# Odd stage of a two-layer trunk: gate products spread through the next projection, as three passes over high and low halves

## The chip, the cores and the metric

The kernel runs on 1 core of one Trainium2 chip. The metric is the device time of one execution in microseconds (us). An engine here is TensorE (PE in the rows, with its weight loads as PEld), VectorE (DVE), ScalarE (ACT), GpSimd (POOL) or SyncE (SP, which issues DMAs). Every engine runs its own instructions in order, and a wait holds back all that stands behind it on that engine.

## What is computed

Two layers follow each other; the change is in the mixer of the second (odd) one, a gated linear recurrence over 1,040 positions and 1,280 channels. `h` is the output of the layer before. Around it stand the even mixer (convolution and sparse attention) and, after each mixer, a routed expert layer and a layer norm; the change leaves them alone.

```python
def rg_lru(xr, w_a, b_a, w_x, b_x, lam):
    xb = xr.reshape(bsz, length, RNN_BLOCKS, RNN_BLOCK_W)          # 10 blocks of 128 channels
    r = sigmoid(einsum('blnc,ncd->blnd', xb, w_a) + b_a)
    i = sigmoid(einsum('blnc,ncd->blnd', xb, w_x) + b_x)
    log_a = -RG_C * r * softplus(-lam)
    a = exp(log_a)
    u = sqrt(-expm1(2.0 * log_a)) * (i * xr)
    ...                                                            # h[n] = a[n] * h[n-1] + u[n]

def rglru_mixer(h, w_in, conv_w, conv_b, w_a, b_a, w_x, b_x, lam, w_out):
    gate, xr = jnp.split(h @ w_in, 2, axis=-1)
    xr = causal_depthwise_conv(xr, conv_w, conv_b)                 # width 4
    y = rg_lru(xr, w_a, b_a, w_x, b_x, lam)
    return (jax.nn.gelu(gate) * y) @ w_out
```

## The kernel before

The stage is `gated_recurrence`. Channels lie on the 128 partitions and positions in the free dimension. The input projection is cut into 20 tiles of 128 output channels (`ODD_TILES`): for each of the 10 channel blocks t one tile of `xr` (s = 1) and one of `gate` (s = 0). Tile 0 is `xr` of block 0, tile 2t+1 is `xr` of block t+1, tile 2t+2 is `gate` of block t. A tile is 72 matmuls of 348 columns: three thirds of the positions, eight pieces of the contraction, and three passes each (`mm3`: high weights by high rows, high by low, low by high), since weights and rows are held as two fp32r halves, high and low.

What each engine does for block t, in the order of its own instructions:

- SP loads the weights of a tile into `raw`, two tiles ahead (line 2323).
- ACT writes the high half of a tile's weights (`split_hi`, line 2364), copies a projected `xr` tile out of PSUM (`take`, line 2373) or runs GeLU on a `gate` tile (line 2375), runs the six sigmoids of the gates (line 2384), then tanh and two exponentials (`decays`, lines 2392 to 2395), and, once DVE has made its input, the square root (`root`, line 2399). It loads an activation table before the first sigmoid, the first exponential, the square root and the GeLU.
- DVE writes the low half of the weights (`split_lo`, line 2432), makes the width-4 convolution of the next block (`conv(t + 1)`, lines 2445 and 2447), then the factor under the root (line 2475, the words below call it e), the product with the gated input (line 2456) and the scan (line 2457).
- POOL multiplies the input gate by the convolved rows (`gated`, line 2485) and the scanned rows by the GeLU output (`out`, line 2490).
- PE projects the tiles in order. After tile 2t+1 stand the gate products of block t (`gates`, line 2345): six matmuls in plain fp32, three thirds of the positions by two gates, from the convolved rows `rg_xc` and the weights `rg_w`. Each waits for the sigmoid two before it, since the PSUM tile `rg_ps` has two buffers. In the trace each of these six stands as two matmul records. Then tile 2t+2 follows.

The order is written out by hand on each engine; nothing reorders it. Semaphores link the engines: `tile_mm` (a tile is projected), `taken` (a tile was copied out), `hi_done` and `lo_done` (weight halves), `conv_d` (convolution done), `gate_mm` and `sig_d` (gate product and sigmoid done), `ix_d`, `h_d`, `y_d`.

Of the kernel before, what the change touches and what calls it, by code (L numbers as in the profile page):

```python
# [14 lines left out]
ALU = mybir.AluOpType  # L15
ACT = mybir.ActivationFunctionType
# [2280 lines left out]
GATE_UNITS = [(j, a0, min(TC, T - a0)) for j in range(2) for a0 in range(0, T, TC)]  # L2297


def gated_recurrence(nc, hT_hi, hT_lo, w_pairs_d, raw, w_loaded, wab, wab_loaded, rp, gate):  # L2300
# [4 lines left out]
    with Ctx(nc) as c:  # L2305
# [3 lines left out]
        sp_, sp8 = c.sb("rg_sp", [P, 3 * RT]), c.sb("rg_sp8", [P, 3 * RT])  # L2309
# [5 lines left out]
            c.sem("rg_" + n) for n in ("cd", "mm", "sg", "ad", "ed", "sq", "ix", "h", "y"))  # L2315
        block = c.block()
# [9 lines left out]
        def _(pe):  # L2326
            def project(n):
                b = n % 2
                pe.wait_ge(lo_done, n + 1)
                if n >= 2:  # L2330
                    pe.wait_ge(taken, n - 1)
                for j in range(3):
                    for k in range(KC):
                        w, m = slice(k * P, (k + 1) * P), slice(j * TC, (j + 1) * TC)
                        last = mm3(pe, ps[b][:, j, 0:TC], (w_hi[:, b, w], w_lo[:, b, w]),
                                   (hT_hi[:, k, m], hT_lo[:, k, m]), k == 0, k == KC - 1)
                last.then_inc(tile_mm, 1)

            def gates(t):
                pe.wait_ge(conv_d, t + 1)  # L2340
                for i, (j, a0, n) in enumerate(GATE_UNITS):
                    u = t * NU + i
                    if u >= 2:
                        pe.wait_ge(sig_d, u - 1)
                    pe.matmul(g_ps[u % 2][:, 0:n], wab[:, j * RT + t, :], xc[:, t % 2, a0:a0 + n], start=True, stop=True
                              ).then_inc(gate_mm, 1)

            project(0)
            project(1)
            pe.wait_ge(wab_loaded, 16)  # L2350
            gates(0)
            for t in range(1, RT):
                project(2 * t)
                project(2 * t + 1) if t + 1 < RT else None
                gates(t)
            project(NT - 1)

        @block.scalar
        def _(act):
# [6 lines left out]
            def take(n):  # L2366
# [7 lines left out]
                else:  # L2374
                    act.activation(gate[:, t, :].rearrange("p (j n) -> p j n", j=3), src, ACT.Gelu_apprx_tanh).then_inc(taken, 1)

# [32 lines left out]
            act.activation(sp_[:, 0:RT], sp_[:, RT:2 * RT], ACT.Ln, bias=1.0).then_inc(lam_d, 1)  # L2409
            take(0)  # L2410
            split_hi(2)
            act.wait_ge(neg_d, 3)
            for t in range(RT):
# [5 lines left out]
                if t + 1 < RT:  # L2419
                    take(2 * t + 1)  # L2420
                    split_hi(2 * t + 3)
                decays(t)
                root(t)
            take(NT - 1)

        @block.vector
        def _(dve):
# [250 lines left out]
```

## Time and profile before

| | |
|---|---|
| median of 3 runs | 2745.87 us (2743.52 to 2746.61) |
| profiled execution, its own time | 2740.98 us |
| its span, first to last instruction | 2739.2 us |
| PE busy, PEld busy | 2470.9 us (90%), 2098.1 us (77%) |
| DVE, ACT, POOL busy | 2015.1 (74%), 1699.7 (62%), 653.5 us (24%) |
| odd stage, in the span | 1575.4 to 1872.2 us |
| mean granted clock of TensorE | 0.943 |

A page of the profile gives, per engine, the share of the span in which it was busy. The span is a chain of stages with different limits, so the averages say little of the odd stage. It is read from windows of its own, from the instructions in order of time, and from the list of who waited for whom. Times in the rows are us from the start of the span; durations of a single matmul overlap those of the next, so the distance between two starts is what a matmul costs in a stream. The other stages take the rest of the span and hold no line that the change touches, but for two small constants whose place in memory moves.

### The profile page before, as it was taken

The page shows a single profiled execution, that of the slowest core. Times are in us where ns is not written, and L with a number is a line of the kernel's source. Part 1 is how long each engine was busy: PE and PEld are TensorE (multiplying, and loading weights), DVE is VectorE, ACT ScalarE, POOL GpSimd, SP SyncE. Part 2 cuts the span into 40 slices and gives each one's busy share as a digit, 9 for nine tenths or more (in the row PEclk, how much of TensorE's full clock was granted, in tenths as well). Part 3 has the DMA queues.
Part 4 walks back from the last instruction along what each step waited for, and adds up shares of the span by engine and source line. Part 5 has one row for each costly group of instructions (what it writes and reads, how often), then busy time and mean ns, then how long its engine had stood idle before and what let it go on. Part 6 is the DMA issues. An engine that isn't in the chain of part 4 may idle for free. (4 is left out here: it accounts for less than half of the span.)

```text
span 2739.2 us, 37516 instructions
## 1 busy us (share of the span) xinstructions
PE 2470.9 (90%) x12571; PEld 2098.1 (77%) x12571; DVE 2015.1 (74%) x2325; ACT 1699.7 (62%) x1800; POOL 653.5 (24%) x484
## 2 busy tenths in 40 slices
PE   8889987998895999999999499997959999999993
PEld 8779966886684888888888388886848888888882
DVE  4677775668658898888988535455469888988895
ACT  2367845666314777777777355554137787787773
POOL 0105716653001212122121311121011222122223
PEclk9899998998996999999999699999969999999996
DMA  5502233322437879998798410103247789999994
GB/s 171 125 1 93 78 96 92 85 57 56 143 116 281 311 262 365 362 382 287 284 368 308 179 47 31 39 24 125 93 171 295 286 294 371 368 365 366 376 355 146
DMA packets 115273, 565.16 MB, mean 206 GB/s; under 512 B 23520, under 2 KB 27872, under 8 KB 65904
## 3 DMA queue, kind: packets, MB, share of 16 engines
q1 hardware_dynamic: 89776, 512.15, 51.2%
q0 software_dynamic: 25408, 51.84, 7.0%
q8 instruction: 53, 0.87, 0.1%
q14 instruction: 36, 0.29, 0.0%
HBM read 574.22 MB, written 74.34 MB: 237 GB/s over the span
## 5 line engine op out<-in xcount | busy, mean ns | idle before, releaser
L1967 DVE TENSOR_TENSOR e0wlo<-e0raw,e0whi 128x2048 fp32r<-128x2048 f32 x214 | 486.7, 2289 | 68.9 <-ACT e0whi L1815 68.8
L1967 DVE TENSOR_TENSOR e1wlo<-e1raw,e1whi 128x2048 fp32r<-128x2048 f32 x208 | 472.8, 2288 | 66.0 <-ACT e1whi L1815 65.8
L1815 ACT ACTIVATE e0whi<-e0raw 128x2048 fp32r<-128x2048 f32 x214 | 409.9, 1916 | 103.8 <-PE e0u L90 42.1
L1815 ACT ACTIVATE e1whi<-e1raw 128x2048 fp32r<-128x2048 f32 x208 | 398.3, 1915 | 101.0 <-PE e1u L90 40.0
L88 PE MATMUL odd_ps<-h2T_hi,odd_w_hi 128*128 128x348 f32 x480 | 158.3, 330 | 6.2 <-DVE odd_w_lo L2432 6.2
L89 PE MATMUL odd_ps<-h2T_lo,odd_w_hi 128*128 128x348 f32 x480 | 155.6, 324 | 0.0
L90 PE MATMUL odd_ps<-h2T_hi,odd_w_lo 128*128 128x348 f32 x480 | 155.3, 324 | 0.0
L88 PE MATMUL m_y<-m_whi,m_xhi 128*128 128x512 f32 (+1 forms) x304 | 121.6, 400 | 21.7 <-DVE m_wlo L1547 21.0
L89 PE MATMUL m_y<-m_wlo,m_xhi 128*128 128x512 f32 (+1 forms) x304 | 119.8, 394 | 0.0
L90 PE MATMUL m_y<-m_whi,m_xlo 128*128 128x512 f32 (+1 forms) x304 | 119.7, 394 | 0.0
L88 PE MATMUL e0g<-e0whi,e0xh 128*128 128x512 f32 x284 | 115.6, 407 | 0.7 <-DVE e0xl L1972 0.7
L88 PE MATMUL e0u<-e0whi,e0xh 128*128 128x512 f32 x292 | 115.6, 396 | 0.0
L89 PE MATMUL e0u<-e0wlo,e0xh 128*128 128x512 f32 x292 | 115.5, 395 | 0.0
L90 PE MATMUL e0u<-e0whi,e0xl 128*128 128x512 f32 x292 | 115.5, 395 | 0.0
L723 ACT ACTIVATE act_junk<-score,cand 128x656 bf16<-128x656 f32 (+2 forms) x96 | 96.8, 1010 | 28.9 <-DVE cand L710 22.5
L2432 DVE TENSOR_TENSOR odd_w_lo<-odd_w_raw,odd_w_hi 128x1024 fp32r<-128x1024 f32 x20 | 28.4, 1423 | 116.6 <-ACT odd_w_hi L2364 116.6
L88 PE MATMUL e0yp<-e0whi,e0hh 128*128 128x512 f32 x280 | 113.8, 407 | 0.0
L88 PE MATMUL e1u<-e1whi,e1xh 128*128 128x512 f32 x284 | 112.4, 396 | 0.0
L90 PE MATMUL e0g<-e0whi,e0xl 128*128 128x512 f32 x284 | 112.3, 396 | 0.0
L89 PE MATMUL e1u<-e1wlo,e1xh 128*128 128x512 f32 x284 | 112.3, 395 | 0.0
L90 PE MATMUL e1u<-e1whi,e1xl 128*128 128x512 f32 x284 | 112.3, 395 | 0.0
L89 PE MATMUL e0g<-e0wlo,e0xh 128*128 128x512 f32 x284 | 112.2, 395 | 0.0
(456 smaller groups left out, 7089.8 us busy)
## 6 DMA issues: line engine op xcount, KB each, us to landing
e0raw<-in_moe_w_gate SPq DMA_DIRECT2D x72, 1024.0 KB
e0raw<-in_moe_w_up SPq DMA_DIRECT2D x72, 1024.0 KB
e0raw<-in_moe_w_down SPq DMA_DIRECT2D x72, 1024.0 KB
e1raw<-in_moe_w_gate SPq DMA_DIRECT2D x70, 1024.0 KB
e1raw<-in_moe_w_up SPq DMA_DIRECT2D x70, 1024.0 KB
e1raw<-in_moe_w_down SPq DMA_DIRECT2D x70, 1024.0 KB
qki_w_raw<-in_w_even SPq DMA_DIRECT2D x22, 512.0 KB, 5.2
odd_w_raw<-in_w_odd SPq DMA_DIRECT2D x20, 512.0 KB, 3.7
```

What stands on the lines that cost most here:

```text
L88: pe.matmul(out, stat[0], mov[0], start=start, stop=False)
L89: pe.matmul(out, stat[0], mov[1], start=False, stop=False)
L90: return pe.matmul(out, stat[1], mov[0], start=False, stop=stop)
L723: act.activation(junk[:, at:at + WIDTH[b]], score[:, AT[b]:AT[b] + WIDTH[b]], ACT.Sign, scale=-1.0, bias=self.cand[:, n:n + 1].bitcast(F32 ...
L1815: act.activation(w_hi[:, i, :], raw[:, i, :], ACT.Copy).then_inc(hi_done[i], 1)
L1967: dve.tensor_tensor(w_lo[:, i, :], raw[:, i, :], w_hi[:, i, :].bitcast(F32), ALU.subtract).then_inc(lo_done[i], 1)
L2432: dve.tensor_tensor(w_lo[:, n % 2, :], raw[:, n % 2, :], w_hi[:, n % 2, :].bitcast(F32), ALU.subtract).then_inc(lo_done, 1)
```

## The change

Two things are done to the gate products of block t, and two tiles are split for it.

- The six products are no longer plain fp32 in a row of their own. Each is now an `mm3` of three fp32r passes, and they stand inside the projection of tile 2t+1: one after every second group of three matmuls, so after groups 2, 4, ... 12 of its 24. For block 0 they stand in tile 1 after groups 14 to 24, for block 9 in tile 19 (the last) after groups 1 to 6. Where block t's products stood behind tile 2t+1 before, they now stand inside it.
- ACT gets `xc_high(t)`: the high half of the block's gate weights (128x256) and of its convolved rows (128x1040). For block t+1 it stands behind `root(t)`, ahead of the GeLU tile.
- DVE gets `xc_low(t)`: two subtractions of 128x128 and one of 128x1040, the low halves. For block t+1 it stands behind the scan of block t, ahead of the low half of the next weights.
- `conv` no longer waits for the gate products of the block two before it but for `xc_high` of it, since that is what reads `rg_xc` now.
- The small tiles `rg_sp` and `rg_sp8` move into unused columns of `const`, and `conv_b` and `lnp` live only in the first layer, which makes room for the four new tiles.

```diff
@@ -2295,9 +2295,10 @@
 
 ODD_TILES = [(0, 1)] + [tile for t in range(RT) for tile in ((t + 1, 1), (t, 0)) if tile[0] < RT]
 GATE_UNITS = [(j, a0, min(TC, T - a0)) for j in range(2) for a0 in range(0, T, TC)]
-
-
-def gated_recurrence(nc, hT_hi, hT_lo, w_pairs_d, raw, w_loaded, wab, wab_loaded, rp, gate):
+GATE_EVERY, FIRST_GATE = 2, 12
+
+
+def gated_recurrence(nc, hT_hi, hT_lo, w_pairs_d, raw, w_loaded, wab, wab_loaded, rp, gate, spare):
 
 
     B_A, B_X, LAM, CB, CW = 0, RT, 2 * RT, 3 * RT, 4 * RT
@@ -2306,13 +2307,16 @@
         w_hi, w_lo = c.sb("odd_w_hi", [P, 2, KC * P], F32R), c.sb("odd_w_lo", [P, 2, KC * P], F32R)
         xr = c.sb("xr", [P, 2, RCONV - 1 + TP])
         xc, a, tt, rr, ii = (c.sb("rg_" + n, [P, 2, T]) for n in ("xc", "a", "t", "r", "i"))
-        sp_, sp8 = c.sb("rg_sp", [P, 3 * RT]), c.sb("rg_sp8", [P, 3 * RT])
+        xc_hi, xc_lo = (c.sb("rg_xc_" + n, [P, T], F32R) for n in ("hi", "lo"))
+        wab_hi, wab_lo = (c.sb("rg_w_" + n, [P, 2, P], F32R) for n in ("hi", "lo"))
+        sp_, sp8 = (spare[:, a * RT:(a + 3) * RT] for a in (0, 3))
         ps = [c.ps(f"odd_ps{s}", [P, 3, 512]) for s in range(2)]
         g_ps = [c.ps(f"rg_ps{s}", [P, 512]) for s in range(2)]
         hi_done, lo_done, tile_mm, taken = (c.sem("odd_" + n) for n in ("hi", "lo", "mm", "taken"))
         lam_d, neg_d, zero_d, chain = (c.sem("rg_" + n) for n in ("lam", "neg", "z", "ch"))
         conv_d, gate_mm, sig_d, act_d, e_d, sq_d, ix_d, h_d, y_d = (
             c.sem("rg_" + n) for n in ("cd", "mm", "sg", "ad", "ed", "sq", "ix", "h", "y"))
+        xc_hi_done, xc_lo_done = (c.sem("rg_" + n) for n in ("xc_hi", "xc_lo"))
         block = c.block()
 
         @block.sync
@@ -2326,6 +2330,7 @@
         def _(pe):
             def project(n):
                 b = n % 2
+                t = 0 if n == 1 else n // 2 if n % 2 else None
                 pe.wait_ge(lo_done, n + 1)
                 if n >= 2:
                     pe.wait_ge(taken, n - 1)
@@ -2334,26 +2339,26 @@
                         w, m = slice(k * P, (k + 1) * P), slice(j * TC, (j + 1) * TC)
                         last = mm3(pe, ps[b][:, j, 0:TC], (w_hi[:, b, w], w_lo[:, b, w]),
                                    (hT_hi[:, k, m], hT_lo[:, k, m]), k == 0, k == KC - 1)
+                        i, between = divmod(j * KC + k + 1 - (FIRST_GATE if t == 0 else 0), 1 if n == NT - 1 else GATE_EVERY)
+                        if t is not None and between == 0 and 1 <= i <= NU:
+                            gate_unit(t, i - 1)
                 last.then_inc(tile_mm, 1)
 
-            def gates(t):
-                pe.wait_ge(conv_d, t + 1)
-                for i, (j, a0, n) in enumerate(GATE_UNITS):
-                    u = t * NU + i
-                    if u >= 2:
-                        pe.wait_ge(sig_d, u - 1)
-                    pe.matmul(g_ps[u % 2][:, 0:n], wab[:, j * RT + t, :], xc[:, t % 2, a0:a0 + n], start=True, stop=True
-                              ).then_inc(gate_mm, 1)
-
-            project(0)
-            project(1)
-            pe.wait_ge(wab_loaded, 16)
-            gates(0)
-            for t in range(1, RT):
-                project(2 * t)
-                project(2 * t + 1) if t + 1 < RT else None
-                gates(t)
-            project(NT - 1)
+            def gate_unit(t, i):
+                j, a0, n = GATE_UNITS[i]
+                if t == 0 and i == 0:
+                    pe.wait_ge(wab_loaded, 16)
+                if i == 0:
+                    pe.wait_ge(xc_hi_done, 2 * t + 2)
+                    pe.wait_ge(xc_lo_done, 3 * t + 3)
+                u, w = t * NU + i, j * RT + t
+                if u >= 2:
+                    pe.wait_ge(sig_d, u - 1)
+                mm3(pe, g_ps[u % 2][:, 0:n], (wab_hi[:, j, :], wab_lo[:, j, :]),
+                    (xc_hi[:, a0:a0 + n], xc_lo[:, a0:a0 + n]), True, True).then_inc(gate_mm, 1)
+
+            for n in range(NT):
+                project(n)
 
         @block.scalar
         def _(act):
@@ -2374,6 +2379,13 @@
                 else:
                     act.activation(gate[:, t, :].rearrange("p (j n) -> p j n", j=3), src, ACT.Gelu_apprx_tanh).then_inc(taken, 1)
 
+            def xc_high(t):
+                act.wait_ge(conv_d, t + 1)
+                if t:
+                    act.wait_ge(gate_mm, NU * t)
+                act.activation(wab_hi[:], wab[:, t:RT + t + 1:RT, :], ACT.Copy).then_inc(xc_hi_done, 1)
+                act.activation(xc_hi[:], xc[:, t % 2, :], ACT.Copy).then_inc(xc_hi_done, 1)
+
             def sigmoids(t):
                 if t >= 2:
                     act.wait_ge(h_d, t - 1)
@@ -2407,8 +2419,10 @@
             act.activation(sp_[:, RT:2 * RT], sp_[:, 0:RT], ACT.Exp, scale=-1.0).then_inc(lam_d, 1)
             act.wait_ge(lam_d, 3)
             act.activation(sp_[:, 0:RT], sp_[:, RT:2 * RT], ACT.Ln, bias=1.0).then_inc(lam_d, 1)
+            act.wait_ge(wab_loaded, 16)
             take(0)
             split_hi(2)
+            xc_high(0)
             act.wait_ge(neg_d, 3)
             for t in range(RT):
                 if t:
@@ -2421,6 +2435,8 @@
                     split_hi(2 * t + 3)
                 decays(t)
                 root(t)
+                if t + 1 < RT:
+                    xc_high(t + 1)
             take(NT - 1)
 
         @block.vector
@@ -2438,7 +2454,7 @@
                 dve.wait_ge(taken, tile + 1)
                 if t >= 2:
                     dve.wait_ge(ix_d, t - 1)
-                    dve.wait_ge(gate_mm, NU * (t - 1))
+                    dve.wait_ge(xc_hi_done, 2 * (t - 1))
                 for j in range(RCONV):
                     src, wj = xr[:, s, j:j + T], rp[:, CW + RT * j + t:CW + RT * j + t + 1]
                     if j == 0:
@@ -2448,6 +2464,13 @@
                     if j < RCONV - 1:
                         ch.link(ins)
                 ins.then_inc(conv_d, 1)
+
+            def xc_low(t):
+                dve.wait_ge(xc_hi_done, 2 * t + 2)
+                for j in range(2):
+                    dve.tensor_tensor(wab_lo[:, j, :], wab[:, j * RT + t, :], wab_hi[:, j, :].bitcast(F32), ALU.subtract
+                                      ).then_inc(xc_lo_done, 1)
+                dve.tensor_tensor(xc_lo[:], xc[:, t % 2, :], xc_hi[:].bitcast(F32), ALU.subtract).then_inc(xc_lo_done, 1)
 
             def scan(t):
                 s = t % 2
@@ -2466,6 +2489,7 @@
             dve.wait_ge(zero_d, 1)
             conv(0)
             split_lo(2)
+            xc_low(0)
             for t in range(RT):
                 if t + 1 < RT:
                     split_lo(2 * t + 3)
@@ -2474,6 +2498,8 @@
                 dve.wait_ge(act_d, 3 * t + 3)
                 dve.scalar_tensor_tensor(tt[:, t % 2, :], rr[:, t % 2, :], 1.0, tt[:, t % 2, :], ALU.add, ALU.mult).then_inc(e_d, 1)
                 scan(t)
+                if t + 1 < RT:
+                    xc_low(t + 1)
                 if t + 2 < RT:
                     split_lo(2 * t + 4)
 
@@ -2506,12 +2532,13 @@
-        cb, lnp, rp = g.sb("conv_b", [P, CG]), g.sb("lnp", [P, 2 * CG]), g.sb("rp", [P, 8 * RT])
+        rp = g.sb("rp", [P, 8 * RT])
+            cb, lnp = c.sb("conv_b", [P, CG]), c.sb("lnp", [P, 2 * CG])
@@ -2580,7 +2607,7 @@
-                gated_recurrence(nc, hT_hi, hT_lo, A["w_odd"], odd_raw, odd_loaded, wab, wab_loaded, rp, gate)
+                gated_recurrence(nc, hT_hi, hT_lo, A["w_odd"], odd_raw, odd_loaded, wab, wab_loaded, rp, gate, const[:, C_PHASE:C_ALL])
```

On PE, before: the end of tile 3 (`xr` of block 2), the gate products of block 1, the start of tile 4.

```order
L90 MATMUL odd_ps1<-h2T_hi,odd_w_lo 128x348
L2345 MATMUL rg_ps0<-rg_xc,rg_w 128x348
L2345 MATMUL rg_ps1<-rg_xc,rg_w 128x348
L2345 MATMUL rg_ps0<-rg_xc,rg_w 128x344
L2345 MATMUL rg_ps1<-rg_xc,rg_w 128x348
L2345 MATMUL rg_ps0<-rg_xc,rg_w 128x348
L2345 MATMUL rg_ps1<-rg_xc,rg_w 128x344
L88 MATMUL odd_ps0<-h2T_hi,odd_w_hi 128x348
```

On PE, now: the start of tile 3, with the gate products of block 1 in it.

```order
L90 MATMUL odd_ps0<-h2T_hi,odd_w_lo 128x348
L88 MATMUL odd_ps1<-h2T_hi,odd_w_hi 128x348
L89 MATMUL odd_ps1<-h2T_lo,odd_w_hi 128x348
L90 MATMUL odd_ps1<-h2T_hi,odd_w_lo 128x348
L88 MATMUL odd_ps1<-h2T_hi,odd_w_hi 128x348
L89 MATMUL odd_ps1<-h2T_lo,odd_w_hi 128x348
L90 MATMUL odd_ps1<-h2T_hi,odd_w_lo 128x348
L88 MATMUL rg_ps0<-rg_xc_hi,rg_w_hi 128x348
L89 MATMUL rg_ps0<-rg_xc_lo,rg_w_hi 128x348
L90 MATMUL rg_ps0<-rg_xc_hi,rg_w_lo 128x348
L88 MATMUL odd_ps1<-h2T_hi,odd_w_hi 128x348
```

The first gate product of block 1 stood behind all 72 matmuls of tile 3 and now stands behind six of them; the other 66 are queued behind its wait.

On DVE, before, one block from the low halves of the weights (`odd_w_lo`) through the convolution (`rg_xc`), e (`rg_t` from `rg_r`), the product (`rg_i`) and the scan (`rg_t` from `rg_a`):

```order
L2432 TENSOR_TENSOR odd_w_lo<-odd_w_raw,odd_w_hi 128x1024 x2
L2445 TENSOR_SCALAR rg_xc<-xr,rp 128x1040
L2447 SCALAR_TENSOR_TENSOR rg_xc<-xr,rp,rg_xc 128x1040 x3
L2475 SCALAR_TENSOR_TENSOR rg_t<-rg_r,rg_t 128x1040
L2456 TENSOR_TENSOR rg_i<-rg_i,rg_t 128x1040
L2457 SCALAR_TENSOR_TENSOR rg_t<-rg_a,rg_i 128x1040
```

On DVE, now:

```order
L2448 TENSOR_TENSOR odd_w_lo<-odd_w_raw,odd_w_hi 128x1024 x2
L2461 TENSOR_SCALAR rg_xc<-xr,rp 128x1040
L2463 SCALAR_TENSOR_TENSOR rg_xc<-xr,rp,rg_xc 128x1040 x3
L2499 SCALAR_TENSOR_TENSOR rg_t<-rg_r,rg_t 128x1040
L2479 TENSOR_TENSOR rg_i<-rg_i,rg_t 128x1040
L2480 SCALAR_TENSOR_TENSOR rg_t<-rg_a,rg_i 128x1040
L2471 TENSOR_TENSOR rg_w_lo<-rg_w,rg_w_hi 128x128 x2
L2473 TENSOR_TENSOR rg_xc_lo<-rg_xc,rg_xc_hi 128x1040
```

The three subtractions for the gate products (`rg_w_lo`, `rg_xc_lo`) stand behind e, the product and the scan, though their input is the convolution ahead of these.

On ACT, now, from the input's copy of a tile (`xr`) to the GeLU:

```order
L2378 ACTIVATE xr<-odd_ps 128x1044
L2369 ACTIVATE odd_w_hi<-odd_w_raw 128x1024
L2404 ACTIVATE rg_t<-rg_r,const 128x1040
L2405 ACT_TABLE_LOAD
L2405 ACTIVATE rg_a<-rg_r,const 128x1040
L2407 ACTIVATE rg_r<-rg_r,const 128x1040
L2411 ACT_TABLE_LOAD
L2411 ACTIVATE rg_t<-rg_t 128x1040
L2386 ACTIVATE rg_w_hi<-rg_w 128x256
L2387 ACTIVATE rg_xc_hi<-rg_xc 128x1040
L2380 ACT_TABLE_LOAD
L2380 ACTIVATE gate<-odd_ps 128x1044
```

(Line numbers of these rows are those of the changed kernel.) Before, the rows of lines 2386 and 2387 were not there, and GeLU's followed the square root. The high halves stand behind the root, which waits for DVE's e.

## Rows read from the trace of the kernel before

**Rows 1.** The page: engine, busy us (share of the span) xinstructions.
```profile
PE 2470.9 (90%) x12571; PEld 2098.1 (77%) x12571; DVE 2015.1 (74%) x2325; ACT 1699.7 (62%) x1800; POOL 653.5 (24%) x484
```

**Rows 2.** Windows: length, busy us (xinstructions) by engine, clock granted, DMA share, GB/s.
```profile
1608.50:1835.10 226.60, 216.37 (x1251) 200.10 (x1250) 112.20 (x72) 133.66 (x145) 43.21 (x15) 1.00 0.11 36
...
1715.60:1744.05 28.45, 27.00 (x158) 24.99 (x157) 14.28 (x9) 16.67 (x18) 5.81 (x2) 1.00 0.11 37
```

**Rows 3.** PE in order of time: start, us, instruction, xcount, [idle before <-releaser].
```profile
1583.16 0.33 PE L88 MATMUL odd_ps<-h2T_hi,odd_w_hi 128*128 128x348 f32 x1
...
1588.42 0.33 PE L88 MATMUL odd_ps<-h2T_hi,odd_w_hi 128*128 128x348 f32 x1
...
1591.78 0.32 PE L88 MATMUL odd_ps<-h2T_hi,odd_w_hi 128*128 128x348 f32 x1
```

**Rows 4.** PE in order of time around gates(3), after gates(0); last weight loads of gates(3), gates(8).
```profile
1687.30 1.33 PE L2345 MATMUL rg_ps<-rg_xc,rg_w 128*128 128x348 f32 x4
1690.03 2.92 PE L2345 MATMUL rg_ps<-rg_xc,rg_w 128*128 128x344 f32 x8 [1.39 <-ACT rg_r L2384]
1692.52 0.58 PE L88 MATMUL odd_ps<-h2T_hi,odd_w_hi 128*128 128x348 f32 x1
1692.94 0.32 PE L89 MATMUL odd_ps<-h2T_lo,odd_w_hi 128*128 128x348 f32 x1
...
1608.48 0.58 PE L88 MATMUL odd_ps<-h2T_hi,odd_w_hi 128*128 128x348 f32 x1
...
1692.10 0.30 PEld L2345 LDWEIGHTS rg_ps<-rg_xc,rg_w 128*128 128x128 f32 x2 [0.29 <-ACT rg_i L2384]
...
1834.37 0.30 PEld L2345 LDWEIGHTS rg_ps<-rg_xc,rg_w 128*128 128x128 f32 x2 [0.29 <-ACT rg_i L2384]
```

**Rows 5.** DVE in order of time, block 0's convolution, then one later block.
```profile
1593.13 0.82 DVE L2445 TENSOR_SCALAR rg_xc<-xr,rp 128x1040 f32<-128x1040 f32 x1 [11.86 <-ACT xr L2373]
1593.98 3.98 DVE L2447 SCALAR_TENSOR_TENSOR rg_xc<-xr,rp,rg_xc 128x1040 f32<-128x1040 f32 x3
1597.88 1.22 DVE L2432 TENSOR_TENSOR odd_w_lo<-odd_w_raw,odd_w_hi 128x1024 fp32r<-128x1024 f32 x1
...
1695.44 1.69 DVE L2432 TENSOR_TENSOR odd_w_lo<-odd_w_raw,odd_w_hi 128x1024 fp32r<-128x1024 f32 x1 [12.81 <-ACT odd_w_hi L2364]
1697.06 2.96 DVE L2445 TENSOR_SCALAR rg_xc<-xr,rp 128x1040 f32<-128x1040 f32 x1
1703.95 1.23 DVE L2475 SCALAR_TENSOR_TENSOR rg_t<-rg_r,rg_t 128x1040 f32<-128x1040 f32 x1
1706.39 1.24 DVE L2456 TENSOR_TENSOR rg_i<-rg_i,rg_t 128x1040 f32<-128x1040 f32 x1 [1.21 <-ACT rg_t L2399]
1707.67 2.32 DVE L2457 TENSOR_TENSOR_SCAN rg_t<-rg_a,rg_i 128x1040 f32<-128x1040 f32 x1
```

**Rows 6.** ACT in order of time: block 0's copy out, then the same later block.
```profile
1591.97 1.04 ACT L2373 ACTIVATE xr<-odd_ps 128x1044 f32<-128x1044 f32 x1 [11.26 <-PE odd_ps L90]
...
1693.43 1.04 ACT L2373 ACTIVATE xr<-odd_ps 128x1044 f32<-128x1044 f32 x1
1694.35 1.06 ACT L2364 ACTIVATE odd_w_hi<-odd_w_raw 128x1024 fp32r<-128x1024 f32 x1
...
1705.22 1.07 ACT L2399 ACTIVATE rg_t<-rg_t 128x1040 f32<-128x1040 f32 x1 [3.77 <-DVE rg_t L2475]
```

**Rows 7.** POOL in order of time, the same later block.
```profile
1693.61 2.44 POOL L2485 TENSOR_TENSOR rg_i<-rg_i,rg_xc 128x1040 f32<-128x1040 f32 x1 [22.64 <-ACT rg_i L2384]
1696.01 3.45 POOL L2490 TENSOR_TENSOR gate<-rg_t,gate 128x1040 f32<-128x1040 f32 x1
...
1869.74 2.38 POOL L2490 TENSOR_TENSOR gate<-rg_t,gate 128x1040 f32<-128x1040 f32 x1 [7.20 <-ACT gate L2375]
```

**Rows 8.** Small operations on DVE and ACT, in order of time.
```profile
1580.75 0.17 DVE L2463 TENSOR_TENSOR rg_sp<-rg_sp 128x10 f32<-128x10 f32 x1 [1.83 <-ACT rg_sp L2409]
...
1578.98 0.21 ACT L2407 ACTIVATE rg_sp<-rg_sp 128x10 f32<-128x10 f32 x1
```

**Rows 9.** SP's queue: the load of the gates' weights.
```profile
1538.06 0.44 SPq L2579 DMA_DIRECT2D rg_w<-in_w_rg  x1
```

**Rows 10.** PE's idle times, and windows of the clock behind the second.
```profile
307.73 0.43 PE L88 MATMUL qkg_ps<-hT_hi,qki_w_hi 128*128 128x348 f32 x1 [3.03 <-POOL qki_w_lo L219]
...
1852.81 4.22 PE L2345 MATMUL rg_ps<-rg_xc,rg_w 128*128 128x344 f32 x8 [4.92 <-ACT rg_r L2384]
...
307.70:312.00 4.30, 4.27 (x27) 4.28 (x28) 3.57 (x13) 4.30 (x7) 1.37 (x1) 1.00 0.97 229
...
1852.80:1856.20 3.40, 3.39 (x6) 1.88 (x7) 0.00 (x0) 1.50 (x3) 0.00 (x0) 0.51 0.00 0
```

## The prediction

> **What bounds the kernel now.** The page of the profile comes first: PE is busy 90% of the span and its weight loads 77% [rows 1], so what lengthens or shortens PE's stream moves the end one for one, unless a wait takes its place. The change lies in the odd stage alone, so windows come next: from block 1's first tile to the end of block 8's gate products the stage takes 226.6 us at a granted clock of 1.00, and one block after another takes 28.45 us, with DVE busy 14.3 and ACT 16.7 of that [rows 2]. Nothing but PE is near its limit over a block. What matters is then the order within a block, so I read the engines in order of time.
>
> PE: eleven groups of three matmuls lie between the two starts at 1583.16 and 1588.42, so one matmul of a stream costs 5.26 / 33 = 0.159 us [rows 3]. A block has 144 of them, 23.0 us. The rest of the 28.45 is the gate products: their first start is 1687.30 and the next tile starts at 1692.52, 5.22 us, and that tile's first matmul takes 0.42 instead of 0.16 to hand over (1692.52 to 1692.94), which makes 5.5 [rows 4]. In them lies one idle time of 1.39 us, behind the first sigmoid.
>
> **The change, part by part.** I call B the start of the matmul behind the last one of tile 2t+1.
>
> *Gate products on PE.* Removed: 5.5 us a block. Added: 6 products of 3 passes, 18 x 0.159 = 2.9 us, taking fp32r passes of 348 columns at the price of the tile's own. If nothing waits, a block is 162 x 0.159 = 25.8 us, 2.6 less than 28.45.
>
> *The wait that goes with it.* The products of block t+1 now stand behind only 72 + 6 matmuls after B, so PE asks for them at B + 78 x 0.159 = B + 12.4. What they need is the last low half of `xc_low(t + 1)`. Its chain, each step from a row:
> - ACT copies the tile out from B + 0.2 (1591.97 against the next tile's start at 1591.78) [rows 3, 6]. The six sigmoids end ahead of B now, so nothing is ahead of it.
> - From the start of the copy to that of DVE's low half of the weights: 1693.43 to 1695.44, 2.0 us, ACT's two operations [rows 5, 6]. B + 2.2.
> - Low half and convolution: in a late block 1695.44 to 1703.95, 8.5 us, e following [rows 5]. Two of these are long because POOL is at work: the low half takes 1.69 against 1.22, the first step of the convolution 2.96 against 0.82, and POOL's product ends at 1696.05 and its next operation at 1699.46 [rows 5, 7]. In the change the sigmoids end some 5 us ahead of B, and POOL's two operations, 2.4 each without a neighbour [rows 7], are over by then. So 8.5 - 0.5 - 2.1 = 5.9. If that cover is gone, the 2.6 come back.
> - e 1.23, root 1.07, product 1.24, scan 2.32: from 1703.95 to the end of the scan at 1709.99, 6.0 us [rows 5, 6]. B + 14.1.
> - `xc_low`: two subtractions of 128x128, between 0.17 (128x10) and 1.22 (128x1024); I take 0.28, on the line between them, as 128 columns are nearer to 10. One of 128x1040 at 1.24, as the product [rows 5, 8]. 1.8 in all, B + 15.9. Bounds: 1.6 to 3.6.
> - The high halves on ACT, a copy of 256 columns between 0.21 and 1.06 (0.45 taken) and one of 1040 at 1.06 [rows 6, 8], end at B + 12: the root ends at B + 10.4, 3.7 before the scan does. They are hidden, until they took over 3.7 us; GeLU and the next weights behind them wait for nothing urgent, as tile 2t+3 ends over 13 us later.
>
> So `xc_low` stands behind the root and the scan of the block before, which it doesn't need, and PE waits from B + 12.4 to B + 16.0, 3.5 us, with 66 matmuls of the tile and 18 passes queued behind that wait. These take 84 x 0.159 = 13.4 and the start after the idle time 0.1: the block is 29.45 us, 1.0 more than before. The 3.5 idle eat the 2.6 won. Within the tile the products then come every 9 matmuls, 1.43 us; the first sigmoid and its table load take some 1.8, against 2.9 until the third product, so no second wait.
>
> *Ends of the stage.* Block 0: the convolution ends at 1597.9 [rows 5], ACT's halves at 1599.5, `xc_low` at 1601.3. PE asks after 42 matmuls of tile 1, 1591.78 + 6.7 = 1598.5: 2.8 idle, then 48 matmuls; tile 2 starts at 1609.1 against 1608.48 [rows 3, 4]: +0.6. The block after it: the last products of block 0 stand at the very end of tile 1, so its last sigmoid, POOL's product and the copy come 1 us late, 30.45. Eight blocks after: 30.45 + 7 x 29.45 = 236.6. Before, tile 18 starts 0.42 after the last weight load of its gate products, as tile 14 does, at 1834.8: 226.3 from 1608.48 [rows 4]. +10.3. Block 9: the products follow after every group, the wait is 4.0 and a second one behind the table load 0.6; its sigmoids, exponentials, root, scan and POOL's last product end 35.8 after B, and before it was 1872.1 - 1834.8 = 37.3 [rows 7]: -1.5. At no cost: the new room in memory; ACT's new wait for the gates' weights, issued 54 us before it needs them [rows 9]; and SP's loads, which wait for DVE's low half of tile 2t+2. That stands behind `xc_low` now and ends at B + 17.1, and the tile it loads for is split over 20 us later.
>
> The sum is +0.6 + 10.3 - 1.5 = +9.4 us.
>
> **The clock.** PE will have ten new idle times: 2.8, 4.5 (block 1, with its late copy), eight of 3.5 to 4.0. The rows have two of that size: after 3.03 idle the granted clock stayed 1.00, after 4.92 it was 0.51 over the next 3.4 us, level 1.2 GHz [rows 10]. Such a fall costs half of 3.4, 1.7 us, and all of it on the path, since PE's tile sets the next block. Ours lie between the two rows. I take two falls, the longest waits, +3.4, and keep none and nine (+15.3) as bounds.
> The Trainium skill ("TensorE: Matmul & The Clock Gate", section "Why this matters for your kernels") warns of idle gaps between bursts of matmuls, since the engine goes back to its lower clock. By that rule every one of our waits but the shortest costs its 1.7 us and the time is that of rival 1; the 3.03 row does not show it and the 4.92 row does.
>
> Against the profiled execution: 2740.98 + 9.4 + 3.4 = 2753.8. It lies 4.9 under the median of the runs, so against the median: 2745.87 + 12.8 = **2758.7 us**, +0.5%.
>
> **Rivals.**
> 1. *The clock falls after nearly every wait.* For it: 3.5 to 4.5 is above 3.03. Against: it is 1.4 under 4.92. Nine falls: 2745.87 + 9.4 + 15.3 = 2770.6, or 2778 if a low stretch is longer than 3.4 us.
> 2. *The products are ready in time, and the change does what it says* (on the other side: faster). The gain is decided at one place, the first product's wait in tiles 3 to 17: the chain must be under 12.4 us instead of 15.9. Then each block is 25.8, 2.6 x 8 = 21 less, 2.4 less in tile 1 and about 5 at the end: 2745.87 - 28 = 2718. For it: only if e, root and scan didn't stand ahead of `xc_low`; they do, and their 6.0 us are measured [rows 5, 6].
> 3. *Wait and gain cancel.* If the chain were 0.9 us shorter, or three waits less exposed, a block stays 28.45 and the time moves within 0.2%: 2745.87 - 1 to + 5. For it: 6 or 7 steps of mine come from a block in which POOL and the sigmoids lay otherwise. Against: all the low ends together take 0.2 off the chain.
>
> **How the numbers follow.** Forecast (no fall to five falls, 2753 to 2765) 0.55; rival 1 (2765 to 2778) 0.20; rival 3 (2741 to 2751) 0.14; rival 2 (about 2718) 0.08; longer still, if the small subtractions go by their upper bound (+1.8 a block), 0.03. A range from 2748 to 2775 leaves out rival 2, about half of rival 3 and the top of rival 1, some 0.2. A measurement of this kernel tells 0.2% (5.5 us) from no change. Faster than that: rival 2 and a little of rival 3, 0.09. Within: 0.13. Slower: 0.78.
>
> **What the changed profile would show.** Right: PE idle 3 to 4 us ahead of the first product in tiles 3 to 17, put down to DVE's low half of the rows; a block of 29 to 30 us; POOL's two operations ahead of the copy; the convolution's first step at 0.8; some windows of clock 0.5 to 0.9 behind these waits, or none. Wrong: no wait at that product and a block near 26 (rival 2), a wait under 2.7 (rival 3), a low clock in each block (rival 1), a long first step of the convolution (POOL's cover gone), or passes in the tile that cost more than 0.159.

## The result and the profile after

| | before | after |
|---|---|---|
| median of 4 runs | 2744.69 us | 2761.28 us (2760.0 to 2764.31) |
| ratio, 95% interval | | 1.0074 (1.0061 to 1.0086) |
| span of the profiled execution | 2739.2 | 2760.0 |
| odd stage, first matmul to POOL's last product | 294.3 | 316.1 |
| one block in the middle of the stage | 28.45 | 30.77 |

The kernel became slower by 0.7%. In the profiled executions the odd stage is 21.8 us longer. The two executions differ elsewhere too: the stage before ends 0.6 us later and the stages behind take 1.7 us less. Over all the profiles below, the odd stage starts between 1574.5 and 1583.2 us though nothing ahead of it differs, so the whole time of a single execution is good to some microseconds. A stage measured within itself is good to about one: its first tile runs in part at a low clock in every profile, for 3.6 to 6.2 us, and that differs from profile to profile. Time and stage stand side by side for that reason.

The page has PE as busy as before [rows 1]; DVE and POOL are a little less busy, ACT 13 us more:

```profile
PE 2471.8 (90%) x12631; PEld 2116.2 (77%) x12631; DVE 2010.1 (73%) x2355; ACT 1713.0 (62%) x1820; POOL 639.9 (23%) x484
```

The windows, with columns as in [rows 2]: from the last product of block 0 to the end of block 8 (block 1's first tile starts 0.5 us into it, at 1609.78), one block, and the 3.4 us and 15.2 us from the start of that block's products.

```profile
1609.31:1857.76 248.45, 221.92 (x1302) 219.89 (x1301) 106.51 (x96) 145.50 (x161) 40.98 (x17) 0.94 0.10 32
1703.95:1734.72 30.77, 27.57 (x165) 27.32 (x164) 13.25 (x12) 18.14 (x20) 4.81 (x2) 0.94 0.10 35
1719.70:1723.10 3.40, 3.37 (x15) 3.40 (x16) 1.07 (x1) 2.23 (x3) 0.00 (x0) 0.66 0.35 105
1719.70:1734.90 15.20, 15.17 (x86) 15.20 (x87) 1.07 (x1) 4.58 (x7) 4.81 (x2) 0.89 0.11 36
```

Where [rows 2] had a granted clock of 1.00 over eight blocks, it is 0.94 now, and 0.66 right behind the wait. PE in order of time in that block:

```profile
1716.22 0.32 PE L90 MATMUL odd_ps<-h2T_hi,odd_w_lo 128*128 128x348 f32 x1
1719.73 0.40 PE L88 MATMUL rg_ps<-rg_xc_hi,rg_w_hi 128*128 128x348 f32 x1 [3.20 <-issue]
...
1721.59 0.49 PE L88 MATMUL rg_ps<-rg_xc_hi,rg_w_hi 128*128 128x348 f32 x1
1721.88 0.49 PE L89 MATMUL rg_ps<-rg_xc_lo,rg_w_hi 128*128 128x348 f32 x1
...
1724.20 0.34 PE L88 MATMUL rg_ps<-rg_xc_hi,rg_w_hi 128*128 128x344 f32 x1
```

The block's tile boundary B is 1703.95. PE runs to 1716.22 + 0.16, asks for the first product at B + 12.4, and gets it at 1719.73, B + 15.8. The list of waits calls the idle time "issue" and names no engine; in `e3_fill` below it puts the same wait down to DVE's low half of the rows, `rg_xc_lo`. At 1721.6 two matmuls are 0.29 us apart, which is the 1.2 GHz level (0.16 at 2.4). DVE and ACT in that block:

```profile
1706.16 1.23 DVE L2448 TENSOR_TENSOR odd_w_lo<-odd_w_raw,odd_w_hi 128x1024 fp32r<-128x1024 f32 x1 [16.16 <-ACT odd_w_hi L2369]
1707.31 0.82 DVE L2461 TENSOR_SCALAR rg_xc<-xr,rp 128x1040 f32<-128x1040 f32 x1
1712.05 1.23 DVE L2499 SCALAR_TENSOR_TENSOR rg_t<-rg_r,rg_t 128x1040 f32<-128x1040 f32 x1
1714.50 1.24 DVE L2479 TENSOR_TENSOR rg_i<-rg_i,rg_t 128x1040 f32<-128x1040 f32 x1 [1.21 <-ACT rg_t L2411]
1715.77 2.32 DVE L2480 TENSOR_TENSOR_SCAN rg_t<-rg_a,rg_i 128x1040 f32<-128x1040 f32 x1
1718.01 0.47 DVE L2471 TENSOR_TENSOR rg_w_lo<-rg_w,rg_w_hi 128x128 fp32r<-128x128 f32 x2
1718.40 1.23 DVE L2473 TENSOR_TENSOR rg_xc_lo<-rg_xc,rg_xc_hi 128x1040 fp32r<-128x1040 f32 x1
...
1714.30 0.40 ACT L2386 ACTIVATE rg_w_hi<-rg_w 128x256 fp32r<-128x256 f32 x1
1714.60 1.06 ACT L2387 ACTIVATE rg_xc_hi<-rg_xc 128x1040 fp32r<-128x1040 f32 x1
```

The last low half ends at 1719.63 and PE starts at 1719.73. Against [rows 5] the first step of the convolution takes 0.82 instead of 2.96: POOL is out of its way, with operations of 2.44 and 2.42 us from 1729.81 to 1734.6, just ahead of the next boundary at 1734.72.

### The profile page after: what moved, and what is told of

Same layout as the page of the kernel before. It is cut to its first block and busy times, and to the rows that moved or that the text cites. A ratio compares the mean times of both kernels' runs of the same rounds, so it can differ in the third digit from the quotient of the medians.

```text
span 2760.0 us, 37696 instructions
## 1 busy us (share of the span) xinstructions
PE 2471.8 (90%) x12631; PEld 2116.2 (77%) x12631; DVE 2010.1 (73%) x2355; ACT 1713.0 (62%) x1820; POOL 639.9 (23%) x484
```

## The experiments

Two theories stood at the start. **A**: PE waits for a chain on ACT and DVE that ends 15.8 us behind the boundary, and each such wait brings PE's clock down, which costs time on top of the wait. **B**: the passes inside a tile cost more than 0.159 us each, or something else slows the 84 matmuls behind the wait; the idle time is only beside it. Each kernel was timed in 3 rounds (the last in 5) against the kernel before on the same chip. "Stage" is again from the first matmul of the odd stage to POOL's last product in the profiled execution: 294.3 before, 316.1 with the change. Times of different rows were taken beside different runs of the kernel before (medians 2739.9 to 2744.7), so the ratio is what to compare.

| kernel | time, us | ratio to before (95%) | stage, us | a block, us |
|---|---|---|---|---|
| the change | 2761.28 | 1.0074 (1.0061 to 1.0086) | 316.1 | 30.75 |
| e1_late | 2725.56 | 0.9942 (0.9925 to 0.9959) | 283.3 | 26.5 |
| e2_halves_first | 2738.11 | 0.9993 (0.9983 to 1.0003) | 292.4 | 27.8, two of 29.3 |
| e3_fill | 2748.18 | 1.0027 (1.0018 to 1.0037) | 303.3 | 29.27 |
| e4_two_later | 2749.27 | 1.0039 (1.0024 to 1.0053) | 305.9 | 28.27 and 29.80 |
| e5_passes_alone | 2742.22 | 1.0002 (0.9989 to 1.0014) | 296.0 | 28.0, one of 29.6 |
| e6_spread_alone | 2721.58 | 0.9929 (0.9911 to 0.9946) | 276.4 | 26.72 |
| e7_first_and_later | 2721.29 | 0.9920 (0.9902 to 0.9938) | 272.8 | 25.77 |
| e8_sigmoids_first | 2728.97 | 0.9948 (0.9929 to 0.9966) | 284.5 | 27.0 |
| e9_all | 2724.86 | 0.9943 (0.9924 to 0.9961) | 278.4 | 27.0 |
| e10_best | 2714.21 | 0.9891 (0.9875 to 0.9908) | 269.0 | 25.77 |

### The clock: fill the wait, or shorten it

`e3_fill` keeps the wait and gives PE something to do in it, FILL = 14 matmuls (code cut):

```diff
+                if i == 0:
+                    if t:
+                        for _ in range(FILL):
+                            pe.matmul(g_ps[u % 2][:, 0:TC], w_hi[:, 1, 0:P], hT_hi[:, 0, 0:TC], start=True, stop=True)
+                    pe.wait_ge(xc_hi_done, 2 * t + 2)
+                    pe.wait_ge(xc_lo_done, 3 * t + 3)
```

> The changed kernel with 14 more matmuls of 348 columns ahead of the wait of each block but the first, into the PSUM tile that the product then overwrites: 2.2 us of work in the idle 3.2 us, used by nobody. Theory (idle time brings the clock down, 1.3 us each in nine blocks): the idle time is 1.0, the clock stays at 1.00, a block of 29.4 us instead of 30.75, time about 2750. Rival (the slow 84 matmuls behind the wait have another cause): the same 30.75 and 2761. If filling delays the product: over 2761.

`e4_two_later` asks for the products two groups, 0.95 us, later:

```diff
-                        i, between = divmod(j * KC + k + 1 - (FIRST_GATE if t == 0 else 0), ...
+                        i, between = divmod(j * KC + k + 1 - (FIRST_GATE if t == 0 else 2), ...
```

> The products of blocks 1 to 9 stand two groups later (4 to 14, and 3 to 8 in the last tile), so PE asks 0.95 us later for the same chain. Theory: idle 2.25 us, the clock stays, a block of 28.45 us, time about 2742. Rival 1 (the clock falls after these waits too): a block of 29.8, about 2753. Rival 2 (the clock plays no part, only the place does): 0.95 a block, about 2753 with a clock of 1.00.

One block of `e3_fill` as a window and the list's line for its ten waits (us in total, times, longest), then two neighbouring blocks of `e4_two_later`:

```profile
1695.22:1724.50 29.28, 28.26 (x179) 28.00 (x178) 13.25 (x12) 18.02 (x20) 4.81 (x2) 1.00 0.12 37
...
PE rg_ps L88 <- DVE rg_xc_lo L2476: 13.2, 10, 2.6
```

```profile
1670.90:1699.16 28.26, 26.01 (x165) 25.75 (x164) 13.26 (x12) 18.03 (x20) 4.83 (x3) 1.00 0.12 38
1699.16:1728.95 29.79, 27.55 (x164) 27.29 (x163) 13.25 (x12) 18.14 (x20) 4.87 (x3) 0.94 0.11 36
```

More work for nothing made the kernel faster by 13 us: with 1.0 us idle instead of 3.2 the clock stays at 1.00 in blocks 2 to 9 and a block takes 29.27 instead of 30.75. So a fall costs 1.5 us, and theory B has no place left: the same passes behind the same chain run at full speed. The 1.5 comes out of the matmuls too: a low stretch of 3.4 us holds about 12 of them at 0.29 us, and 12 x (0.29 - 0.159) = 1.6. `e4_two_later` was expected to have no falls at an idle time of 2.25; it has them in about every second block, and the pair above shows the same 1.5 (29.79 against 28.26). So the time came out between the 2742 of the theory and the 2753 of rival 1, and what failed is the idea that 2.25 us are short enough.

Over the odd stages of all twelve profiles, PE's idle times by size and how many of them had a fall of the clock in or within 2 us behind them: 0.9 to 1.0 us, none of 24; 1.4 to 1.5, 2 of 17; 1.8 to 1.9, 3 of 8; 2.2 to 2.4, 5 of 9; 2.6 to 2.8, 6 of 10; 3.2, 8 of 8; over 3.6, 4 of 4. In these runs the share with a fall grows with the idle time. The Trainium skill ("TensorE: Matmul & The Clock Gate", section "Why this matters for your kernels") has it as a rule to keep such gaps short; the trace of the change agrees, with all nine waits of 3.2 us and more, and the shorter waits of `e4_two_later` show that it can strike earlier. The wait of 3.03 us in another stage, which had none [rows 10], stands in all twelve profiles at 2.9 to 3.0 us, in code that is the same in all of them but for places in memory. Eight of the twelve have a fall at it, and the kernel before is one of the four that have none. In `e1_late`, PE's row and the clock behind it:

```profile
303.94 0.43 PE L88 MATMUL qkg_ps<-hT_hi,qki_w_hi 128*128 128x348 f32 x1 [3.01 <-POOL qki_w_lo L219]
...
305.40:308.90 3.50, 3.50 (x14) 3.50 (x13) 2.97 (x9) 3.50 (x7) 2.03 (x1) 0.51 0.83 236
```

The clock falls at the same wait in one execution and not in another, so a single row without a fall could not tell that a wait of that size is safe.

### The place: ask later

`e1_late` has the products of every block at groups 14 to 24 (block 9: 10 to 15).

```diff
-                        i, between = divmod(j * KC + k + 1 - (FIRST_GATE if t == 0 else 0), ...
+                        i, between = divmod(j * KC + k + 1 - (FIRST_GATE if n < NT - 1 else 9), ...
```

> Only the place of the gate products changes: behind groups 14 to 24 of a tile for every block (as for block 0), behind groups 10 to 15 in the last tile. Theory (PE waits for a chain that ends 15.8 us behind the tile boundary, and a wait over 3 us brings the clock down): the products now come 18 us behind the boundary, so no wait and no low clock in blocks 1 to 8, a block of 25.8 us, time about 2724. Rival (the passes inside a tile cost more than 0.159 us, which would explain the 15.0 us behind the wait as well): no wait, but a block of 27.3, about 2736. If the late sigmoids push the next chain back by more than 2 us: a wait again, about 2745.

The direction and most of the size came: 14.4 us faster than before, and by the ratios 36 us under the change. But a block takes 26.5 and 0.5 us of wait are left, not 25.8 and none. DVE and POOL in one block (B = 1685.11) show why:

```profile
1688.24 1.69 DVE L2448 TENSOR_TENSOR odd_w_lo<-odd_w_raw,odd_w_hi 128x1024 fp32r<-128x1024 f32 x1 [9.29 <-ACT odd_w_hi L2369]
1689.86 2.96 DVE L2461 TENSOR_SCALAR rg_xc<-xr,rp 128x1040 f32<-128x1040 f32 x1
...
1686.41 2.44 POOL L2511 TENSOR_TENSOR rg_i<-rg_i,rg_xc 128x1040 f32<-128x1040 f32 x1 [20.67 <-ACT rg_i L2396]
1688.80 3.45 POOL L2516 TENSOR_TENSOR gate<-rg_t,gate 128x1040 f32<-128x1040 f32 x1
```

The products at the tile's end push the sigmoids over the boundary. POOL then runs beside the next convolution, the long 1.69 and 2.96 of [rows 5] are back, the price that the prediction had named for the lost cover, and the chain ends 19.2 us behind B instead of 15.8.

### The queues: take the halves ahead

`e2_halves_first` leaves the products where the change has them and moves the halves ahead of the root and of the scan.

```diff
                 decays(t)
-                root(t)
                 if t + 1 < RT:
                     xc_high(t + 1)
+                root(t)
...
-                scan(t)
                 if t + 1 < RT:
                     xc_low(t + 1)
+                scan(t)
```

> The products stay where the change put them; ACT's high halves move ahead of the root and DVE's low halves ahead of the product and the scan. Theory: the chain ends 11.2 us behind the boundary instead of 15.8, PE asks at 12.4, no wait in blocks 1 to 8 and hardly one in block 9, a block of 25.8 us, the 2.6 us wait of block 0 stays, time about 2720. Rival (the order on DVE does not matter, another wait is behind PE's): still 3 us idle and about 2761.

The wait for the rows' low half is gone in blocks 1 to 9, as the theory had it (the low half ends at B + 11.3), but the time is that of before (the interval of the ratio, 0.9983 to 1.0003, includes 1). The list of PE's waits in the odd stage names another engine (us in total, times, longest):

```profile
PE rg_ps L88 <- ACT rg_r L2396: 17.2, 9, 2.7
```

PE's row and ACT's queue ahead of it, in one block (B = 1696.93):

```profile
1714.14 0.42 PE L88 MATMUL rg_ps<-rg_xc_hi,rg_w_hi 128*128 128x344 f32 x1 [1.76 <-ACT rg_r L2396]
```

```profile
1706.56 1.28 ACT L2411 ACT_TABLE_LOAD   x1
1707.85 1.08 ACT L2411 ACTIVATE rg_t<-rg_t 128x1040 f32<-128x1040 f32 x1
1708.94 1.28 ACT L2380 ACT_TABLE_LOAD   x1
1710.24 1.04 ACT L2380 ACTIVATE gate<-odd_ps 128x1044 f32<-128x1044 f32 x1
1711.18 1.05 ACT L2369 ACTIVATE odd_w_hi<-odd_w_raw 128x1024 fp32r<-128x1024 f32 x1
1712.24 1.28 ACT L2396 ACT_TABLE_LOAD   x1
1713.54 0.99 ACT L2396 ACTIVATE rg_r<-rg_ps,rp 128x348 f32<-128x348 f32 x2
```

The first product is computed at B + 12.4, but ACT has no idle time from the high halves on and reaches the first sigmoid at B + 16.6; the third product waits for that. The first wait had hidden a second one, 1.8 us long. Two kernels tell whether it is ACT's queue. `e8_sigmoids_first` puts the sigmoids ahead of the GeLU tile:

```diff
+                sigmoids(t)
                 if t:
                     take(2 * t)
                     if t + 1 < RT:
                         split_hi(2 * t + 2)
-                sigmoids(t)
```

> e2_halves_first with ACT's six sigmoids ahead of the GeLU tile and its weight half; products at groups 2 to 12 as in the change. Theory (ACT's queue): the first sigmoid no longer stands behind 3.4 us of GeLU and weights, it ends 14.9 us behind the boundary, the third product is asked for at 15.3, so no wait, no low clock, 25.8 a block, about 2714. Rival (ACT is short of time as such, since a table load may come on top): a wait stays at the third product or ahead of the next tile, 27 us a block, about 2730.

`e7_first_and_later` keeps ACT's order and asks six groups later (8 to 18) in blocks 1 to 8:

```diff
-                        i, between = divmod(j * KC + k + 1 - (FIRST_GATE if t == 0 else 0), ...
+                        i, between = divmod(j * KC + k + 1 - (FIRST_GATE if t == 0 else 0 if n == NT - 1 else 6), ...
```

> e2_halves_first with the products of blocks 1 to 8 six groups later (8 to 18). In e2 the wait was ahead of the third product, for the first sigmoid, which ACT reached 16.6 us behind the boundary, after the high halves, root, GeLU, a weight half and two table loads. Theory (ACT's queue is the next one late): the third product is asked for at 18.1 us, past the first sigmoid's end at 17.2, so no wait in blocks 1 to 8 and a block of 25.8 us; POOL's two operations end just as DVE's next block starts, 0 to 0.6 us. About 2717. Rival (the waits come with the order itself): 27.8 a block as in e2, about 2737.

Both took the wait for the sigmoid away in blocks 1 to 8. `e7_first_and_later` then has none in blocks 1 to 8, and six of its blocks, as one window, are PE from end to end, at the price forecast:

```profile
1665.63:1820.23 154.60, 154.60 (x974) 154.60 (x974) 82.72 (x72) 108.94 (x120) 28.96 (x13) 1.00 0.12 38
```

154.6 / 6 = 25.77 us. Its median is 4 us over the expected 2717, which its four times (2718.0 to 2725.0) do not settle; the profiled execution is the slowest of them, and its odd stage starts 4 to 9 us later than that of the others. `e8_sigmoids_first` shows a third wait behind the second. PE, DVE and POOL, around the boundary at 1716.80:

```profile
1717.87 0.43 PE L88 MATMUL odd_ps<-h2T_hi,odd_w_hi 128*128 128x348 f32 x1 [0.91 <-DVE odd_w_lo L2448]
...
1715.15 2.67 DVE L2448 TENSOR_TENSOR odd_w_lo<-odd_w_raw,odd_w_hi 128x1024 fp32r<-128x1024 f32 x1 [9.68 <-ACT odd_w_hi L2369]
...
1714.32 2.42 POOL L2516 TENSOR_TENSOR gate<-rg_t,gate 128x1040 f32<-128x1040 f32 x1
```

The weight half that stood ahead of the sigmoids now comes behind them, its low half meets POOL's product (2.67 us instead of 1.2, ending 1.1 us behind it), and the next tile waits 0.9 us for its weights. 27.0 a block is what the rival said, by another route than its table load.

### The two halves of the change by themselves

`e5_passes_alone` has the halves and the three passes, in a row behind the tile as before. `e6_spread_alone` is the kernel before with its fp32 products spread as in the change, and no halves. The edit of `e5_passes_alone` (code cut):

```diff
-                        i, between = divmod(...)
-                        if t is not None and between == 0 and 1 <= i <= NU:
-                            gate_unit(t, i - 1)
                 last.then_inc(tile_mm, 1)
+                if t is not None and n < NT - 1:
+                    for i in range(NU):
+                        gate_unit(t, i)
+                if n == NT - 2:
+                    for i in range(NU):
+                        gate_unit(RT - 1, i)
```

> The changed kernel with its gate products in a row of their own behind tile 2t+1, as before the change; halves and three passes stay. Theory: the row is held by the first sigmoid and its table load, not by the passes, so the 5.5 us of the row become about 5.2 and the time is 2742, with 2.5 us idle in the row. Rival (passes are the gain: 0.58 to 0.48 a product and no slow hand-over): 0.9 a block, about 2736.

That of `e6_spread_alone`, against the kernel before (code cut; `project` calls `gate_unit` as in the change):

```diff
+            def gate_unit(t, i):
...
+                if i == 0:
+                    pe.wait_ge(conv_d, t + 1)
...
+                pe.matmul(g_ps[u % 2][:, 0:n], wab[:, j * RT + t, :], xc[:, t % 2, a0:a0 + n], start=True, stop=True
+                          ).then_inc(gate_mm, 1)
```

> The kernel before with its plain fp32 products spread through the tile at the places of the change, no halves. Theory: no wait, since the convolution ends 8 us behind the boundary; each product costs 0.58 us and 0.26 for the hand-over to the next fp32r matmul, 5.1 us a block against 5.5 in a row, and the tail is a little shorter: about 2738. Rival (in a stream fp32 costs no hand-over and the whole row's wait is won): a block of 26.5, about 2727.

One block of each:

```profile
1685.69:1713.71 28.02, 26.34 (x165) 25.76 (x164) 15.88 (x12) 17.77 (x20) 5.86 (x2) 1.00 0.12 38
```

```profile
1687.17:1713.89 26.72, 26.72 (x159) 25.22 (x158) 11.70 (x9) 16.77 (x18) 4.82 (x2) 1.00 0.13 40
```

The passes alone bring nothing: the row behind a tile is held by the first sigmoid and its table load (1.51 us idle ahead of the third product), so a block goes from 28.45 to 28.0, and the end of the stage takes that back: block 9's products wait 6.3 us for their halves, and the clock falls there too. The spread alone brings 20 us, where 2738 would have been 2 to 7 us under the medians of before. I had charged each fp32 product 0.58 us plus 0.26 for the hand-over, 5.1 a block; in the tile it is (26.72 - 144 x 0.159) / 6 = 0.64, 3.8 a block. And it needs only the convolution, which is there by B + 8, so none of the waits of the other kernels arises but 0.9 us in block 1 and 0.5 in block 9. A three-pass product costs (25.77 - 22.9) / 6 = 0.48, so the passes are worth 0.16 x 6 = 1 us a block, where they find no wait. Both prices are whole passes: 0.48 is three times the 0.159 of one fp32r matmul, 0.64 is four times.

### The version that beats both

`e9_all` is `e8_sigmoids_first` with block 0's products in plain fp32, waiting for the convolution alone. `e10_best` does the same to `e7_first_and_later`, and puts the sigmoids ahead of the GeLU for block 9 alone.

```diff
-                if i == 0:
-                    pe.wait_ge(xc_hi_done, 2 * t + 2)
-                    pe.wait_ge(xc_lo_done, 3 * t + 3)
+                if i == 0 and t == 0:
+                    pe.wait_ge(conv_d, 1)
+                elif i == 0:
+                    pe.wait_ge(xc_hi_done, 2 * t)
+                    pe.wait_ge(xc_lo_done, 3 * t)
...
+                if t == 0:
+                    pe.matmul(g_ps[u % 2][:, 0:n], wab[:, w, :], xc[:, 0, a0:a0 + n], start=True, stop=True).then_inc(gate_mm, 1)
+                    return
```

> e8_sigmoids_first, and block 0's products in plain fp32 without halves, so that they wait for the convolution alone. Theory: the 2.6 us wait in tile 1 goes, 0.9 us come back as six fp32 products cost 0.62 instead of 0.48 each: 1.7 less than e8, about 2712. Rival (the wait in tile 1 was hidden behind block 1's chain): as e8.

> e7_first_and_later (blocks of 25.77 us without a wait) with its two remaining waits treated: block 0's products in plain fp32, which wait for the convolution alone, and in block 9 the sigmoids ahead of the GeLU of block 8. Theory: the 2.6 us ahead of block 0's products become about 1 us of dearer products, and the 2.7 us ahead of the last tile's third product go with their low clock; the odd stage takes 268 to 269 us instead of 272.8, the time is 4 us under e7's: about 2717. Rival (both waits are hidden behind ACT's chain at the end of the stage): as e7, 2721.

`e9_all` shortens the stage by 6.2 us, more than the 1.7 expected. The 6.8 us of low clock at block 0's wait in `e8_sigmoids_first` are gone with it, worth 6.8 x (1 - 0.159 / 0.29) = 3.1 us, and the low clock at the start of its first tile is 2.4 us shorter, worth another 1.1, a difference between the two executions and not between the kernels. In `e10_best` all that is left of PE's waits between the odd stage's products is 0.5 us:

```profile
PE rg_ps L88 <- ACT rg_r L2401: 0.5, 1, 0.5
```

Its stage takes 269.0 us, as expected, and its time is 2714.21 us, by the ratios 1.1% under before and 1.8% under the change.

## Why the prediction was right, and where not

The forecast was 2758.7 us, in a range of 2748 to 2775, slower with a chance of 0.78; the time is 2761.28. The case that came true is rival 1 in its mechanism (the clock falls after nearly every wait) at a time that lies within the forecast. The waits were forecast well; the nearness of the whole time is in part luck, as the last points show.

- **The price of a block without a wait**, 25.8 us: right, 25.77 in `e7_first_and_later`.
- **The wait**: right to 0.1 or 0.2 us. PE asks at B + 12.4 (12.4); the chain ends at 15.7 (15.9), with the two small subtractions at 0.47 together (0.56), POOL out of the convolution's way and the high halves hidden, both as forecast.
- **The block with the wait but a full clock**, 29.45: `e3_fill` has 29.27. Block 1: 30.45 forecast. With the change it took 32.7 (1609.78 to 1642.44), of which a low clock of 6.8 us, worth 3.1 as above, is more than the whole excess: without it some 29.6.
- **The first block**: 2.8 idle forecast, 2.64 measured.
- **The clock**: the term that was mis-sized. I took two falls at 1.7 us from two rows, 3.4 us in all. There were nine, one behind each wait from block 1 on, at 1.5 us each in blocks 2 to 8: from 29.27 to 30.75. The first, 6.8 us long, cost 3.1, and the one in block 9 some 0.7, an estimate: from its products to the end block 9 takes 21.0 us in the change and 20.3 in `e3_fill`, where no fall follows. That makes about 14 of the 21.8 us that the stage lost. The waits, less what the shorter products gave back, are the rest, about 7.5 where I had 9.4. `e3_fill` agrees: almost without falls it is 0.27%, 7.4 us, over before. The step that failed is the reading of [rows 10]: one idle time without a fall and one with it were taken as two ends between which most of ours would be spared, when all nine of those were above the first (3.2 to 4.1 us), and the first was itself a wait at which most executions have a fall (eight of twelve profiles). Nor is a fall worth half of 3.4 us: matmuls go from 0.159 to 0.29 us and not to twice 0.159.
- **That the time is nonetheless near**: the stage grew by 21.8 in the profiles and the medians by 16.6. The difference of 5.2 can be counted: outside the stage the changed kernel's profile is 1.0 shorter, the profiled execution before, at 2740.98, lies 3.7 under the median of the four, and that of the change 0.5 over its own. So the sum, 12.8, was 9 us short of the stage, and chance in single executions took 5 of the 9 back. The other three executions of the change do not look as if they had fewer falls: their granted clocks over the whole kernel are 0.937 to 0.939, against 0.940 in the profiled one, though this counts the other stages too. The start of the odd stage goes with the clock ahead of it: over the twelve profiles the low clock before it sums to 180 us (start at 1574.5) up to 214 us (1578.9 and 1583.2), with a correlation of 0.84; what else moves the start stays open.
- **Rival 2**, 2718 if the products were ready in time: its time was about right for the kernels that make it so (2721 and 2714; `e10_best` also treats blocks 0 and 9), but the text put the decision on one place, the chain ahead of the first product. `e2_halves_first` took 4.4 us off that chain and came out level with before, because ACT's first sigmoid, which I had passed as "no second wait", was the next one late: I had worked it out for products that come at B + 16, and not for products at 12.4.

## What to carry to other kernels

Work that is moved into an engine's stream is asked for earlier, and its inputs must move up in every queue that makes them. Before such a move, work out for each engine when its part would be ready with the others' waits gone: here a first wait (DVE's low halves), a second (ACT's sigmoids) and a third (a weight half beside POOL) lay behind each other, and asking later was simpler than reordering. A wait that PE had not had before costs its length and, in these runs, with a chance that grew from 2 in 17 at 1.5 us to 8 in 8 at 3.2, another 1.5 us for the clock. One row without a fall does not show that a size is safe, so look at the same wait in several executions. The cheapest test is to fill the wait with work that nobody uses. And of two things done at once, try each alone: the spread was worth 20 us without the three passes, the passes nothing without the spread.

## What the runs showed of the hardware

- The clock does not need a wait of one certain size to fall: it did in 2 of 17 idle times of 1.4 to 1.5 us, in 5 of 9 of 2.2 to 2.4, in all 8 of 3.2. At one wait of 3.0 us in another stage, the same in all twelve profiles, it fell in eight. A low stretch of 3.4 us behind such a wait cost 1.5 us. In the change the falls came in every block in a row, 30.7 us apart, with the same place in each.
- A plain fp32 product of 348 columns costs 0.64 us in a stream of fp32r matmuls, less than its two records of 0.29 and the 0.26 hand-over seen in a row of its own had let me expect (0.84), and four times the 0.159 of one fp32r matmul.
- A DVE subtraction of two fp32 operands in SBUF took 1.2 us alone, and 1.65 (`e7_first_and_later`), 1.69 and 2.67 us where it met a POOL operation; each of these ended 1.1 us behind the end of POOL's.
